# A linear recurrence of 512 tokens in chunks of 64 instead of 32, each chunk prepared by itself

## What is computed

```python
def rwkv7_recurrence(r, log_w, k, v, kk, a, s0):
    def step(s, inp):
        r_t, lw_t, k_t, v_t, kk_t, a_t = inp
        s_kk = jnp.einsum('bhik,bhk->bhi', s, kk_t)
        s = (s * jnp.exp(lw_t)[:, :, None, :]
             - s_kk[..., :, None] * (kk_t * a_t)[..., None, :]
             + v_t[..., :, None] * k_t[..., None, :])
        return s, jnp.einsum('bhij,bhj->bhi', s, r_t)
    ...
```

## Time and profile before

| | us |
|---|---|
| median of 3 runs | 2081.32 (2080.29 to 2083.05) |
| profiled execution, its own time | 2076.66 |
| its span | 2074.9 |
| recurrence in it, from the first L2056 (1156.9) to the first L2415 (1453.9) | 297.0 |
| of that TensorE busy | 214.4 |
| first preparation (1156.9 to 1197.6) | 40.7 |
| products of the two layers, line L329, share of the chain of waits | 59% |

### The profile page before, as it was taken

One profiled execution on the slowest core, in us unless ns is written; L12 is line 12 of the kernel. 1 busy time (PEld: TensorE's weight loads), 2 busy tenths in 40 slices (PEclk: granted clock), 3 DMA queues, 4 the chain that ended last, 5 costly groups with the idle time before them and its releaser, 6 DMA issues.

```text
span 2074.9 us, 47908 instructions
## 1 busy us (share of the span) xinstructions
PE 1834.3 (88%) x21171; PEld 1708.4 (82%) x21171; DVE 1026.3 (49%) x1438; ACT 720.8 (35%) x923; POOL 128.7 (6%) x152
## 2 busy tenths in 40 slices
PE   4999977999999999957989767768889999999996
PEld 3999874999999999936868666657379999999996
DVE  5377766544334444566685433322464443444443
ACT  3353355254322224223453121211435451222333
POOL 1032450000000000000000000000100000000000
PEclk8999988999999999978999766665699999999998
DMA  3321131433322232211212100010024333233321
GB/s 100 81 72 52 52 103 29 112 113 91 101 72 81 81 105 69 72 42 31 82 54 71 33 4 4 4 23 25 0 65 124 88 91 94 61 91 91 92 72 43
DMA packets 237101, 138.61 MB, mean 67 GB/s; under 512 B 6560, under 2 KB 232160, under 8 KB 236944
## 3 DMA queue, kind: packets, MB, share of 16 engines
q1 hardware_dynamic: 226528, 114.31, 19.0%
q0 software_dynamic: 4048, 13.67, 2.7%
q10 hardware_dynamic: 6368, 8.24, 1.2%
HBM read 128.04 MB, written 8.16 MB: 66 GB/s over the span
## 4 chain that ended last, share of the span: by engine, by line
PE 76%; DVE 13%; ACT 4%; issue 4%; POOL 1%; DMA 1%; ACTq 0%; DVEq 0%; POOLq 0%
PE ps L329 59%; PE ps L2080 2%; PE ps L2074 1%; PE ps L1498 1%; DVE w_rest L298 1%; PE ps L1700 1%; ACT w_head L293 1%; PE ps L2232 1%; DVE x_split L1751 1%; PE ps L2241 1%; PE ps L2056 1%; POOL mix L855 1%; PE ps L964 1%; PE ps L2257 1%; PE ps L2217 1%
## 5 line engine op out<-in xcount | busy, mean ns | idle before, releaser
L329 PE MATMUL ps<-x_split,w_head 128*128 128x272 f32 (+1 forms) x5568 | 946.3, 293 | 51.5 <-DVE x_split L1751 20.8
L329 PEld LDWEIGHTS ps<-x_split,w_head 128*128 128x128 f32 x5568 | 801.5, 192 | 72.2 <-issue 48.4
L329 PE MATMUL ps<-x_split,w_rest 128*128 128x272 f32 (+1 forms) x2784 | 582.8, 291 | 0.0
L329 PEld LDWEIGHTS ps<-x_split,w_rest 128*128 128x128 f32 x2784 | 442.7, 192 | 0.0
L293 ACT ACTIVATE w_head<-w_raw 128x1024 fp32r<-128x1024 f32 (+1 forms) x206 | 228.3, 1108 | 605.5 <-PE ps L329 595.1
L298 DVE TENSOR_TENSOR w_rest<-w_raw,w_head 128x1024 fp32r<-128x1024 f32 (+1 forms) x206 | 268.3, 1303 | 193.2 <-ACT w_head L293 193.1
L329 PE MATMUL ps<-hidden_split,w_head 128*128 128x272 f32 x1408 | 233.2, 287 | 0.0
L329 PEld LDWEIGHTS ps<-hidden_split,w_head 128*128 128x128 f32 x1408 | 198.0, 188 | 0.0
L329 PE MATMUL ps<-hidden_split,w_rest 128*128 128x272 f32 x704 | 145.3, 287 | 0.0
L329 PEld LDWEIGHTS ps<-hidden_split,w_rest 128*128 128x128 f32 x704 | 110.1, 188 | 0.0
L1330 DVE TENSOR_TENSOR hT<-hT,ps 128x544 f32<-128x544 f32 (+1 forms) x40 | 28.8, 721 | 161.1 <-PE ps L329 161.1
(11 more groups left out here) (390 smaller groups left out, 1993.3 us busy)
## 6 DMA issues: line engine op xcount, KB each, us to landing
w_raw<-in_w_ffn_gate SPq DMA_DIRECT2D x44, 512.0 KB, 3.8
w_raw<-in_w_ffn_up SPq DMA_DIRECT2D x44, 512.0 KB, 3.8
w_raw<-in_w_ffn_down SPq DMA_DIRECT2D x32, 704.0 KB, 4.6
w_raw<-in_w_in_even SPq DMA_DIRECT2D x29, 512.0 KB, 3.8
w_raw<-in_w_ple_gate SPq DMA_DIRECT2D x16, 512.0 KB, 4.0
w_raw<-in_w_out_even SPq DMA_DIRECT2D x8, 512.0 KB, 4.0
w_raw<-in_rw_wr SPq DMA_DIRECT2D x8, 512.0 KB, 4.1
w_raw<-in_rw_wk SPq DMA_DIRECT2D x8, 512.0 KB, 3.9
```

The lines of the kernel that those rows point to most:

```text
L329: mm = pe.matmul(ps[:, 2 * s + h, 0:half.stop - half.start], w[:, s, k * P:(k + 1) * P], x[:, k, half], start=first and k == 0, stop=k == ...
```

## The change

1. The prompt's chunks have `CP = 64` tokens. There are 8 instead of 16; the sample group keeps its 32-row form. The inverse is 64 x 64 with six levels; level 1 is made without products, so five pairs P, X are left.
2. The log decays are taken relative to the middle of each chunk: VectorE subtracts, after the r products, the sum at token 32 from the first half (`half{t}`, `mid{t}` in `dve_r`), and the state's decay factors get the exponentials of those sums (`halves`, `decays`).
3. All products of the preparation and most of a chunk are 64 x 64: four quarters of the array by turns (`tile_heads`). The output and state sums use all 128 rows and 64 columns (L2383, L2388), the second score product 64 rows and 128 columns ("O", L2109).
4. One chunk is prepared at a time. The preparation ("stream") has 15 parts: aT, five pairs P and X, A, O, vt, kt. Each part on TensorE waits until the part before it has been read out, also where it doesn't need its data; the banks are 6 and 7 for even chunks, 0 and 1 for odd ones. Between the steps of chunk n come 3, 4, 2 parts of chunk n + 1, and behind it the rest.
5. The masks of the levels are applied by GpSimd (`level_mask`), not by VectorE; the upper half of X is copied to the other partitions by ScalarE (`other_rows`, two copies a level).
6. The states st0 and st1 are turned at the end of chunk 6's stream, st2 to st7 in the sample group's.
7. Around it: the rows of keys and queries are laid out by 64, a second table (`odd_levels`, 128 x 384) is loaded by ScalarE's queue, the gate's weights lie elsewhere.

```diff
+CP = 64
+NCP = TP // CP
+LEVELSP = 6
...
+                first = qrF[:, t, :, 0:TP].rearrange("p s (n h t) -> p s n h t", h=2, t=CO)[:, :, :, 0, :]
+                half = wc[:, t // 4, t % 4, 0:NCP]
+                dve.tensor_copy(half, first[:, 1, :, CO - 1]).then_inc(*O1.dve.done(f"half{t}"))
+                dve.wait_ge(*O1.dve.at(f"half{t}"))
+                dve.tensor_tensor(first, first, half.unsqueeze(1).unsqueeze(3).to_broadcast([P, 2, NCP, CO]),
+                                  ALU.subtract).then_inc(*O1.dve.done(f"mid{t}"))
...
+            act.dma_start(odd_levels[:, :], a["odd_levels"]).then_inc(*O0.dma.loaded("levels"))
...
+            parts = [("aT", 0)] + [(kind, level) for level in range(2, LEVELSP + 1) for kind in "PX"]
+            parts += [("A", 0), ("O", 0), ("vt", 0), ("kt", 0)]
+            return parts + [("st", 0), ("st", 1)] if m == SAMPLE - 2 else parts
...
+        def in_chunk(streams, n, slot):
+            for _ in range((3, 4, 2, 0)[slot]):
+                if n + 1 in streams:
+                    next(streams[n + 1], None)
+            if slot == 3:
+                for _ in streams.get(n + 1, ()):
+                    pass
...
+                if before is not None:
+                    for by in readers(*before):
+                        pe.wait_ge(*(O2.act if by == "act" else O2.dve).at(part_name(*before)))
...
+                elif kind == "O":
+                    for i, p, c in tile_heads:
+                        mm = pe.matmul(bank(c)[:, (2 * i + p) * CP:(2 * i + p + 1) * CP], rows_p[half(c), 2 * i + p, P * m:P * m + P],
+                                       qrF[half(c), 2 * i + p, 1, tokens], start=True, stop=True)
...
+        def level_mask(pool, m, level):
+            view = lambda ap: ap.rearrange("p (n t) -> p n t", t=CP)
+            pool.tensor_tensor(view(bTs[m % 2][level % 2]), view(aTs[m % 2]),
+                               lvP[:, level - 1, :].unsqueeze(1).to_broadcast([P, 8, CP]), ALU.mult).then_inc(
+                *O2.pool.done(f"b{m}_{level}"))
...
+            act.wait_ge(*O2.pe.at(f"o{n}"))
+            if n < SAMPLE:
+                act.wait_ge(*O2.dve.at(f"h{n}"))
```

More of the change, by code:

```diff
@@ L118, in odd_tables, with level_masks @@
     batch = [s // ST == np.arange(NB)[None, :]]
-    return np.concatenate([scan_resets(CO), same_head] + halves + prompt + sample + head + batch, 1).astype(np.float32)
+    return np.concatenate([scan_resets(CO), same_head] + level_masks(2, CO) + sample + prompt + head + batch, 1).astype(
+        np.float32)
+def level_masks(levels, block):
+    p, t = np.arange(P)[:, None], np.arange(block)[None, :]
+    s = p % block
+    masks = []
+    for level in range(1, levels + 1):
+        m = 1 << (level - 1)
+        masks.append((s // (2 * m) == t // (2 * m)) & (s % (2 * m) < m) & (t % (2 * m) >= m))
+    return masks
 def head_spread():
@@ L2039, in pe_prepare, with all_chunks, pe_stream @@
+        def all_chunks(eng, stream, chunk):
+            streams = {m: stream(eng, m) for m in range(SAMPLE + 1)}
+            for _ in streams[0]:
+                pass
+            for n in range(SAMPLE + 1):
+                chunk(eng, n, lambda slot: in_chunk(streams, n, slot))
+        def pe_stream(pe, m):
+            if m == 0:
                 for s in range(2):
@@ L2243, in pe_chunk @@
-                mm.then_inc(*O2.pe.done(f"oR{n}"))
-            go_on(preparation, 2)
+                for i, p, c in tile_heads:
+                    mm = pe.matmul(ps[half(c ^ p), 4 + p, 256 + i * CP:256 + (i + 1) * CP], hst[half(c), 2 * i + p, :],
+                                   qrF[half(c), 2 * i + p, 1, tokens], start=i == 0, stop=False, skip_group_check=True)
+                mm.then_inc(*O2.pe.done(f"oR{n}"))
+            go_on(1)
+            pe.wait_ge(*O2.act.at(f"R{n}"))
+            pe.wait_ge(*O2.dve.at(f"X{n}_{LEVELSP}"))
@@ new lines, in pe_chunk @@
+            pe.wait_ge(*O2.act.at(f"U{n}"))
+            pe.wait_ge(*O2.dve.at(f"U{n}"))
+            pe.wait_ge(*O2.dve.at(f"O{n}_0"))
+            pe.wait_ge(*O2.act.at(f"kt{n}_0"))
+            if n > 0:
+                pe.wait_ge(*O2.pe.at(f"oR{n}"))
+            for i, p, c in tile_heads:
+                g = c ^ p
+                pe.matmul(ps[half(g), 4 + p, 256 + i * CP:256 + (i + 1) * CP], vu[:, i, p, g, :],
+                          sO[:, 512 * c + (2 * i + p) * CP:512 * c + (2 * i + p + 1) * CP], start=n == 0 and i == 0, stop=True,
+                          skip_group_check=True)
```

762 lines of the change are left out of this document (416 added, 346 removed).

## The result

The changed kernel took **2148.82 us** in the median of 4 runs (2143.47 to 2155.87), the kernel before 2080.81 us on the same chip: a ratio of 1.033, 95% interval 1.030 to 1.037. It is slower by 68 us. The forecast was 2133 us, with a range from 2093 to 2168. The profiled execution of the changed kernel took 2147.39 us, with a span of 2145.4.

A forecast was written before the change was run, and what follows sets the result against it. TensorE, busy for 88% of the span, was to wait more often in the recurrence: 361.6 - 25 (clock) + 7 (pauses) + 4 (masks) = 347.6 us against 297.0; with plus 1 outside and 4.7 for the median, 2133 us, range 2093 to 2168.

The forecast's parts named there:

- The stage: The recurrence, from first preparation to sample group: 347.6 us forecast against 297.0 before, plus 50.6.
- The walk: Step-by-step sum of the recurrence's chain at TensorE's lower clock, 39.6 us a full chunk: 361.6 us in all.
- O on two row halves: Second score product, 32 instructions: 1.9 us if two halves run together, 4.3 if not; 0 taken, bounds 0 to plus 19.
- GpSimd's masks: Level masks on GpSimd beside VectorE's operations: 0.5 us a stream, plus 4 (0 to 17); by the skill's rule plus 8.
- Clock: TensorE at its upper clock level for a 30% share in the recurrence: minus 25 us, bounds 0 to minus 50.
- Waits of TensorE: TensorE's waits between a chunk's dependent steps, for VectorE, ScalarE and handing over: 14.5 us a chunk.
- pauses: TensorE's pauses called "issue" in the recurrence: 1 us a chunk, plus 7 (0 to 22).
- Tail: Chunk 7 with the sample group's stream 38.6 us and the sample chunk 7.9: 46.5 us.
- First preparation: The recurrence's first stream, TensorE 18.1 us of work and 16 of waits: 34.1 us against 40.7 before.
- Outside: Outside the recurrence: midpoint subtractions hidden, a short VectorE piece a unit and one more transfer on ScalarE: plus 1 us.
- the second: Rival: row halves don't run together, VectorE and GpSimd take turns, clock stays at 0.50: 2190 us; chance 0.08.
- the first: Rival: TensorE's denser stretches hold the upper clock throughout, recurrence 277 us, 2062 us, faster; chance 0.12.

The follow-up runs named there:

- o_quarters: The changed kernel with the second score product O as 64 x 64 products on four quarters instead of 64 x 128 on two row halves: 2136.8 us.
- act_first: The changed kernel with ScalarE copying the sixth level's P before it takes the chunk's output: 2128.6 us.
- woven: The changed kernel with A, O, vt, kt moved between the levels and into the idle bank pair, 5, 5, 3 parts between a chunk's steps: 2051.6 us.
- filled: The changed kernel with extra TensorE products of constants, read by nothing, in nearly all waits of a stream: 2105.2 us.
- woven_all: The order and banks of woven plus the edits of o_quarters and act_first: 2039.79 us, ratio 0.981 to the kernel before.

## Why the prediction was right, and where its terms were off

The direction, the place and the size were right: 2133 us forecast, 2149 measured, 16 above the forecast and inside the range. The stage was to take 347.6 us and took 368.8. The walk gave 361.6 us at the lower clock; this is how it becomes 368.8:

- **O on two row halves: 0 taken, plus 14.4 measured** (1.8 us for each of eight streams). This is the term that failed most clearly. The forecast took the price of two *quarters* by turns for two row halves; the nearer row was the eight transposes on one row half, whose bound of 4.3 us almost holds: 3.68. `o_quarters` won back 12 us (10 by the ratios). The rule of the Trainium skill that was weighed there ("Tiling Modes" in TensorEngine Tiling (Array Packing), two tiles for 64 x 128) would have kept it at 1.9; these products show no such overlap.
- **GpSimd's masks: plus 4 taken, plus 7.7 measured**: 0.94 in each of seven streams (the subtraction 1.63 for 0.69), and 1.09 in the first, where VectorE's mask was the one that met GpSimd's (1.78 for 0.69). The rule weighed there ("SBUF: two separate sides" in SBUF — State Buffer, in the Trainium skill) gave plus 8 and was right; the trace agrees with 1.63 us for L2232 beside GpSimd's 1.77.
- **Clock: minus 25 taken, minus 17 measured.** By the granted clock of 0.58 TensorE was at the upper level for 16% of the chunks, and for none of the first preparation (0.50), not for 30%. The walk's TensorE time in the chunks is seven times 25.1, 2.2 for st0 and st1, and seven times the 1.08 of U, which the walk counted among the waits and left out of the clock's sum: 185.5. With O's extra 12.6 that is 198.1; 181.5 was measured: minus 16.6. The share came from a kernel with longer stretches of work; the text itself bounded it at 0 and minus 50.
- **Waits of TensorE: right but for 4.4 us, with the pauses in them (plus 7 taken).** The walk had 14.5 us a chunk, 13.4 without U; seven of them, 1.6 with st0 and st1 and the mask's 6.6 make 102.1, and 106.5 was measured, 0.5 of it as pauses ("issue"). P to X was 0.80, X to P 1.33, aT to P 3.91 (3.0 and the mask's 0.94), X6 2.4 (1.9 expected: 0.6 + 0.2 + 1.1), vt 1.39 (1.5).
- **Tail: right.** 46.5 expected, 43.8 measured, with st4's load waited for 1.72 us (1.7) and the small products at 7.01.
- **First preparation: right but for O and the masks.** 34.1 and 1.8 and 1.1 make 37.0, which was measured.
- **Outside: plus 1 taken, minus 1 measured.**

Together 361.6 + 14.4 + 7.7 - 16.6 + 4.4 (waits) - 2.7 (tail) = 368.8. In part the closeness is luck. O, the masks and the clock together came out 26.5 us above what was taken for them; the waits with the pauses, the tail, the work outside and the distance of the median from the profiled execution (4.7 taken, 1.4 measured) came out 11 below. Of the rivals, the second was nearest (its first two mechanisms came true, the third in part); the first, with its upper clock in dense stretches, did not come about, though its mechanism is real: with the small waits filled or removed the clock reached 0.80 to 0.84.

What the prediction did not see is that its two largest terms hang together. It priced the waits at their length and the clock by itself. In the runs a small wait costs its length and a part of the clock: `act_first` gave 17 to 20 us where 11 were expected, `woven` took 38 us off TensorE's busy time with the same products, and `filled` gained 44 by adding work. So the change is slower because of its order of parts, its bank pair and, for 10 to 12 us, the tiles of O, not because chunks of 64 are dear: with the same chunks, `woven_all` is 109 us faster. Whether the kernel before, whose clock in the recurrence was 0.50 to 0.67, would gain by the same means was not tried, so nothing here shows that chunks of 64 are the better choice. What decides where the clock rises and falls was not settled beyond this; the runs tell that the many waits of 0.5 to 2.4 us count, and that filling the one of 3.9 us pays little while they are open.

## What to carry to other kernels

When a change shortens the list of independent parts between dependent steps, count TensorE's waits and price each above its length, since here small waits also lost the clock for what followed; try the cheapest test first, filling them with products that nobody reads. Before trusting that two tiles of the array run together, look for a row with exactly those tiles, and take the nearest row's bound if there is none. A mask moved to GpSimd isn't free beside a VectorE operation with both inputs in SBUF (1.63 us for 0.69), while beside VectorE's transposition, with one input, both kept their times (0.71 and 1.27); moving one operation away moved the collision to the next.

## What the runs showed of the hardware

- 64-row, 128-column float32 products on two row halves by turns, each half with its own bank: 32 in 3.68 us (115 ns each) at the lower clock. The same sums as 64 x 64 on four quarters: 64 in 1.97 to 1.99 us (31 ns). On 128 rows and two column halves (L2383 in the change) 32 took 1.97 us. One row half alone, with eight transposes, took 1.08 us; without the last instruction's own length that is 109 ns from one to the next, and 105 on the two row halves by turns. So at this clock column halves overlapped and row halves did not.
- VectorE's subtraction of 128 x 512 with both inputs in SBUF: 0.69 us alone, 1.63 beside GpSimd's mask, which took 1.77 where it took 1.27 elsewhere. Both engines lose. Beside VectorE's transposition (one input) GpSimd's mask took 1.27 and the transposition 0.71, as alone.
- With TensorE busy for 69% of a window the granted clock was 0.65 in one kernel and 0.80 in another; the difference was which waits were filled, and how many products that took (68 and 116 a stream).
